# Self attention of a two-block transformer kernel: the difference of two probability maps formed ahead of the turn on VectorE, in place of products with scaled identities on TensorE

## The reference

```python
def one_block(args):
    q_blk, i = args
    sc = jnp.einsum("bhcqd,bhckd->bhcqk", q_blk, k).astype(jnp.float32) * scale
    qpos = i * Q_BLOCK + jnp.arange(Q_BLOCK)
    mask = kpos[None, :] <= qpos[:, None]
    sc = jnp.where(mask, sc, -jnp.inf)
    p = jax.nn.softmax(sc, axis=-1)
    a = p[:, :, 0] - lam * p[:, :, 1]
    return jnp.einsum("bhqk,bhkv->bhqv", a.astype(v.dtype), v)
```

## Time and profile before

| | us |
|---|---|
| median of 3 runs | 2945.64 |
| lowest and highest run | 2942.72, 2948.58 |
| the profiled execution, its own time | 2947.96 |
| its span in the profile | 2946.2 |
| busy: TensorE, VectorE, ScalarE, GpSimd | 2858.0, 2019.0, 1037.2, 1740.7 |

### The profile page before, as it was taken

How to read it: one execution, slowest core, us unless ns; L and a number is a source line. 1 busy time by engine, 2 the same in 40 slices (tenths; PEclk the granted TensorE clock), 3 DMA queues, 4 the chain that set the end, 5 groups by cost and what they waited for, 6 DMA issues and landing times.

```text
span 2946.2 us, 40618 instructions
## 1 busy us (share of the span) xinstructions
PE 2858.0 (97%) x15350; PEld 2547.8 (86%) x15350; DVE 2019.0 (69%) x3386; ACT 1037.2 (35%) x1972; POOL 1740.7 (59%) x997
## 2 busy tenths in 40 slices
PE   6999999999999999999999999999999989999999
PEld 5777778888788777778878889999999989999999
DVE  6985459996352634666647589999898956666663
ACT  3153232121122422333341223333356654444443
POOL 4646447767655235521116667888844558778875
PEclk9999999999999999999999999999999999999999
DMA  4222223333332122210003338999977879999994
GB/s 143 86 66 92 79 65 93 94 100 93 93 115 86 36 61 90 84 39 15 22 23 127 102 99 285 339 329 335 324 256 278 297 262 340 338 344 343 342 342 170
DMA packets 196211, 502.87 MB, mean 171 GB/s; under 512 B 15408, under 2 KB 93488, under 8 KB 194480
## 3 DMA queue, kind: packets, MB, share of 16 engines
q1 hardware_dynamic: 73008, 262.64, 27.4%
q0 software_dynamic: 36864, 134.23, 12.1%
q10 hardware_dynamic: 86144, 103.39, 10.4%
HBM read 448.82 MB, written 51.38 MB: 170 GB/s over the span
## 4 chain that ended last, share of the span: by engine, by line
PE 76%; DVE 14%; issue 3%; POOL 2%; ACT 2%; DMA 2%; DVEq 0%; ACTq 0%; SPq 0%; POOLq 0%
PE banks L1745 20%; PE banks L1747 20%; PE banks L1746 20%; DVE sb_sq L2458 4%; PE banks L1029 3%; PE banks L890 2%; POOL sb_wL L1730 2%; PE banks L898 1%; DVE sb_tmp L2468 1%; DVE sb_sq L2456 1%; PE banks L1807 1%; PE banks L1781 1%; PE banks L1783 1%; PE banks L1782 1%; DVE sb_hL L641 1%
## 5 line engine op out<-in xcount | busy, mean ns | idle before, releaser
L1712 POOL TENSOR_TENSOR sb_wL<-sb_raw,sb_wH 128x1024 fp32r<-128x1024 f32 x242 | 589.0, 2434 | 862.5 <-PE banks L1747 815.0
L1745 PE MATMUL banks<-sb_hH,sb_wH 128*128 128x512 f32 (+1 forms) x2040 | 760.7, 373 | 11.4 <-issue 2.3
L1730 POOL TENSOR_TENSOR sb_wL<-sb_raw,sb_wH 128x1024 fp32r<-128x1024 f32 x253 | 609.4, 2409 | 270.8 <-PE banks L1747 264.7
L1747 PE MATMUL banks<-sb_hH,sb_wL 128*128 128x512 f32 (+1 forms) x2040 | 740.8, 363 | 0.0
L1746 PE MATMUL banks<-sb_hL,sb_wH 128*128 128x512 f32 (+1 forms) x2040 | 740.4, 363 | 0.0
L1745 PEld LDWEIGHTS banks<-sb_hH,sb_wH 128*128 128x128 f32 x2040 | 385.0, 189 | 61.9 <-issue 13.2
L1747 PEld LDWEIGHTS banks<-sb_hH,sb_wL 128*128 128x128 f32 x2040 | 384.3, 188 | 41.0
L1746 PEld LDWEIGHTS banks<-sb_hL,sb_wH 128*128 128x128 f32 x2040 | 385.2, 189 | 38.9 <-issue 1.7
L1194 ACT ACTIVATE sb_wH<-sb_raw 128x1024 fp32r<-128x1024 f32 x253 | 267.9, 1059 | 262.2 <-DMA sb_raw<-in_weights 198.7
L1745 PE MATMUL banks<-sb_pz,sb_wH 128*128 128x384 f32 x1024 | 343.3, 335 | 7.2 <-DVE sb_pz L1650 7.2
L1746 PE MATMUL banks<-sb_pz,sb_wH 128*128 128x384 f32 x1024 | 343.0, 335 | 0.0
(11 more groups left out here) (467 smaller groups left out, 5223.6 us busy)
## 6 DMA issues: line engine op xcount, KB each, us to landing
sb_raw<-in_weights SPq DMA_DIRECT2D x495, 512.0 KB
acts<-sb_sq ACTq DMA_DIRECT2D x120, 192.0 KB
gates<-sb_stage ACTq DMA_DIRECT2D x12, 1920.0 KB, 8.5
sb_Ga<-acts ACTq DMA_DIRECT2D x30, 768.0 KB, 8.3
sb_Gt<-gates ACTq DMA_DIRECT2D x30, 768.0 KB
acts<-sb_xT ACTq DMA_DIRECT2D x1, 2048.0 KB, 7.8
sb_xT<-acts ACTq DMA_DIRECT2D x1, 2048.0 KB, 10.2
out_xT<-sb_xT ACTq DMA_DIRECT2D x8, 256.0 KB, 2.4
```

Of the source, the lines that this page charges most:

```text
L1712: nc.gpsimd.tensor_tensor(wL[:, t % LOS, :], raw[:, t % RAWS, :], wH[:, t % HIS, :].bitcast(F32), ALU.subtract).then_inc(sems("weights_lo" ...
L1730: nc.gpsimd.tensor_tensor(wL[:, t % LOS, :], raw[:, t % RAWS, :], wH[:, t % HIS, :].bitcast(F32), ALU.subtract).then_inc(sems("weights_lo" ...
L1745: pe.matmul(out, hi, H, start=start, stop=False)
L1747: return pe.matmul(out, lo, H, start=False, stop=stop)
```

## The change

The turn no longer scales and adds. ScalarE scales the first map in place by its reciprocal. VectorE multiplies the second reciprocal by the weight `sc[:, 6:7]`, and then forms in place the first map plus the second map times that number. TensorE turns the result block by block with `nc.tensor.transpose` (the helper `turn`). The scaled identities and `lam_ident` go. ScalarE's scaling counts on `probs`, so the counts that others wait for become 3 a unit; two small functions give them.

```diff
+        def exponentials_of(u):
+
+            return 3 * u + 1 if u else 2
+
+        def scaled_of(u):
+
+            return min(3 * u + 5, 48)
...
                 def scores(u):
                     h, i = units[u]
-                    E.at("probs", 2 * (u - 1))
+                    E.at("probs", exponentials_of(u - 2) if u >= 2 else 0)
...
                         for kb in range(units[u][1] + 1):
-                            for c in range(2):
-                                mm = nc.tensor.matmul(ps[6][:, kb * P:(kb + 1) * P], B["p"][:, u % 2, c, kb * P:(kb + 1) * P],
-                                                      B["att"][:, u % 2, c * P:(c + 1) * P], start=(c == 0), stop=(c == 1))
+                            mm = turn(ps[6][:, kb * P:(kb + 1) * P], B["p"][:, u % 2, 0, kb * P:(kb + 1) * P])
...
                     E.wait("recip")
-                    E.at("blocks_turned", u - 1)
-                    act.activation(B["att"][:, u % 2, 0:P], ident, ACT.Copy, scale=ss[:, u % 2, 6:7])
-                    act.activation(B["att"][:, u % 2, P:2 * P], lam_ident, ACT.Copy, scale=ss[:, u % 2, 7:8]).then_inc(sems("att"), 1)
+                    first_map = B["p"][:, u % 2, 0, 0:P * (i + 1)]
+                    act.activation(first_map, first_map, ACT.Copy, scale=ss[:, u % 2, 6:7]).then_inc(sems("probs"), 1)
...
-                v.tensor_scalar(lam_ident, ident, sc[:, 6:7], None, ALU.mult)
...
                     taps(SPLIT + 3 * u, SPLIT + 3 * u + 1)
                     o = u % 2
-                    E.wait("probs", 2)
-                    E.at("att", u - 1)
-                    v.reciprocal(ss[:, o, 6:8], ss[:, o, 4:6]).then_inc(sems("recip"), 1)
+                    E.at("probs", exponentials_of(u))
+                    chain(v.reciprocal(ss[:, o, 6:8], ss[:, o, 4:6]))
+                    v.tensor_scalar(ss[:, o, 7:8], ss[:, o, 7:8], sc[:, 6:7], None, ALU.mult).then_inc(sems("recip"), 1)
                     taps(SPLIT + 3 * u + 1, SPLIT + 3 * u + 3)
+                    E.at("recip", u + 1)
+                    E.at("probs", scaled_of(u))
+                    maps = [B["p"][:, o, c, 0:P * (i + 1)] for c in range(2)]
+                    v.scalar_tensor_tensor(out=maps[0], in0=maps[1], scalar=ss[:, o, 7:8], in1=maps[0], op0=ALU.mult,
+                                           op1=ALU.add).then_inc(sems("att"), 1)
```

More of the change, by code:

```diff
@@ L685, in sb_in @@
             return ps[first + min(kb, 2)][:, at:at + qw[kb]]
-        lam_ident = dg[:, 1, S - P:S]
         parts = [(2, slice(offs[2], 1280), slice(0, 1280 - offs[2])), (1, slice(offs[1], offs[2]), slice(0, qw[1])),
@@ L1988, in _ @@
                         h, i = n // TB, n % TB
-                        E.at("probs", 32 + n - 2)
+                        E.at("probs", 48 + n - 2 if n >= 2 else 0)
                         for b in range(2):
@@ L2382, in _ @@
                 chain(v.tensor_tensor(tmp[:, 0, :], tmp[:, 0, :], tmp[:, 1, :], ALU.add))
+                E.n["probs"] = 48
                 E.meet()
```

## The result

| us | before | after |
|---|---|---|
| median of 10 runs | 2945.53 | 2962.30 |
| lowest and highest run | 2939.21, 2948.76 | 2950.89, 2965.12 |
| the profiled execution, its own time | 2947.96 | 2962.46 |
| its span | 2946.2 | 2960.7 |

The changed kernel is slower by a factor of 1.0052, 95% interval 1.0039 to 1.0064, and its median lies above the range of 2945 to 2957. Two of the ten, 2950.89 and 2951.20, lie near the forecast of 2950.2; the other eight took 2958 or more.

The account below looks back on a forecast made before the run. TensorE was taken to bound the self attention, VectorE after the change. 0.55 plus 4.0 us for meetings with GpSimd made +4.6: 2952.6 for the profiled execution, 2950.2 after 2.3 less for the median; range 2945 to 2957.

Parts of the forecast that it names:

- VectorE becomes the bound: Self attention: with the combinations VectorE needs 16.66 us a head, what TensorE took before, so the gain is eaten.
- the 40 turns: Self attention, TensorE: 160 passes go, 40 turns of 0.112 us come; 17.9 us become 4.5, 13.4 less.
- VectorE's steps: Between one combination's end and the next's start: 4.01 us for i = 2; 3.48, 3.75, 3.21 for i = 0, 1, 3.
- The meetings: Combinations with i = 2 stand behind GpSimd's subtraction L1712: +1.12 us each, +0.67 in unit 14, together 4.0 us.
- The row: Trace reading that L641 ended 0.55 us behind GpSimd's subtraction; kept over the exclusive lock, which would add 0.8 us in sum.
- a head's 16.78 us: Self attention before the change: a head of four units costs 16.78 us, all of it TensorE's.
- The forecast's own sign of being wrong: Wrong if a head takes under 16.5 us, i = 0 combinations are stretched, or the clock leaves 1.00 after 162 us.
- +4.6: Whole change: 0.55 us at the next stage's opening product plus 4.0 for meetings with GpSimd.
- the edges 0.55: Reckoning from first combination to next stage's opening product, meetings left out: 226.15 instead of 225.60, +0.55 us.
- I had taken nothing: ScalarE's scaling as a link in units with i = 1: taken as nothing, 0.2 us a head at most.
- the clock rival: Clock falls after TensorE's waits in i = 2 units: 0.5 x 4 = 2 us more, 2952.2; chance 0.14.
- second meeting at i = 0: Rival: combinations with i = 0, 0.6 us later, also fall behind L1712; 8.5 us for three heads, 2958.7; chance 0.12.

Follow-up runs that it names:

- e4: Changed kernel, with identity products nobody reads filling TensorE's waits only from unit 13 on and ahead of the meeting of engines; 2951.14 us.
- e2: Changed kernel, with identity products nobody reads filling TensorE's waits in every unit but the first two and at the stage's end; 2952.71 us.
- e1: Changed kernel, with the combination reading its second input from the tap sum's PSUM bank, leaving the first map out of the result; 2956.97 us.
- e11: Kernel before the change, with ScalarE held up by fourteen waited-for copies ahead of its last copy of turned blocks, in unit 15; 2958.99 us.
- e10: As e9, but with the other form of the combination for units i = 1 and i = 3, same fills; 2944.24 us.
- e12: As e9, but without its filling products; 2949.01 us, ratio 1.0009 to the kernel before.
- e9: Kernel before, i = 3 alone: VectorE adds the second map, ratio-weighted, to the first; TensorE turns by one scaled identity; tail filled; 2942.31 us.
- e3: Kernel before, with the new scaling, combination and turn for units i = 3 alone, the others keeping scaled identities; 2946.74 us.

## Why the prediction was wrong

**Right.** VectorE becomes the bound; the 40 turns; VectorE's steps. From the start of one combination to the next with i = 2 are 187.30 - 182.81 = 4.49 us, and 4.50 were forecast; for i = 3 to i = 0 it is 4.23 in both. A head that meets GpSimd once is 18.08 us long (192.18 to 210.26); 17.8 was forecast, and 0.30 of the difference is a wait for ScalarE's scaling. The meetings come with i = 2 and not with i = 0, 1.65 to 1.67 us long. The combination of 384 columns ended 0.41 us after the subtraction; by the exclusive lock of the Trainium skill (SBUF — State Buffer, "Who interferes with whom") its full 0.62 would have followed. The row decides for the shorter time, as it did ahead. One reading was a little too strong, without a consequence for the sum: a head's 16.78 us before were not all TensorE's, since 1.5 us of the chain in it lie on ScalarE (exponentials 0.87, scalings 0.59).

The forecast's own sign of being wrong, a clock that leaves 1.00 after 162 us, came true as well.

**The account up to the opening product**, +8.3 where +4.6 was forecast:
- three combinations with i = 2 at 1.66 for 0.62 and unit 14's at 1.05: 3.1 + 0.4 = 3.5 (forecast 4.0);
- the edges 0.55, taken over from the forecast: they are what closes the sum, and were not measured apart;
- unit 1's combination (163.72) stood behind the write of the high part (L1714, 163.50 to 164.55) and took 1.10 for 0.48: 0.6, not forecast;
- three waits of the combination for ScalarE's scaling, 0.30, 1.08 and 0.58: 2.0. I had taken nothing, 0.2 a head at most. They go with the low clock (1.8 in e4, none in e2), though e1 has it for less long and none of them. The way from the one to the other is my reading, not measured: a late TensorE makes scores and turned blocks late, ScalarE's copies with them, and the scaling stands behind those;
- the last products, from the end of unit 15's combination to the opening product, 4.88 us where 3.28 was forecast, at a clock of 0.50: 1.6. At full clock e4 takes 3.85 here, with idle products ahead of the last values, so 1.0 of the 1.6 is shown to go with the clock.

Sum 3.5 + 0.55 + 0.6 + 2.0 + 1.6 = 8.3. The last two, 3.6 us, I put down to the clock.

**The failed step** is the clock rival's "0.5 x 4 = 2 more, 2952.2", and with it the sum's silence on everything behind the opening product. I saw the fall coming, named it with a chance of 0.14, and priced it inside the stage alone, against the microsecond that TensorE is ahead of VectorE there. Inside the stage that was nearly the right size, 2.0 in waits, but partly by luck: they were waits for ScalarE's scaling, which I had priced at nothing; and 1.6 at the end I had not counted. The large price lay where TensorE is the bound again. The stage ends on three units in which it has next to nothing to do, the next one opens at 0.50, and its sums and products keep that for another 20 us: 9.7 us, which e4 took away to within 0.1 by filling the last units, and e11 made from nothing in the old kernel (6.8). With it the forecast would have been 2950.2 + 9.7 = 2959.9, near the measured 2962.3. The two runs of the changed kernel at 2951 would fit executions that did not pay this price; no profile was taken of one.

**Which rivals held.** No second meeting at i = 0. A clock that "falls after each of these waits" is nearly right, but the waits needed no meeting: e1 has none and loses the clock. What stays open is why one execution loses the clock under the opening sums (e10, e12, briefly e1 and e2) and another does not (the kernel before, e9): for the changed kernel the runs show that filling makes it rarer (e2, e4), not when it is safe. What in the next stage keeps the clock down for 20 us was not tried.

## What to carry to other kernels

When work is taken off the engine that is the bound, look past the end of the stage: the granted clock of TensorE in the stretch behind is part of the price, and a tail that leaves it idle can cost more there than all that was saved (here 13.4 us of TensorE's work removed, 16.8 us lost). Cost a clock that falls where TensorE is the bound, not where it waits anyway. And when one engine's spare time (2.7 us a head here) is to take over another's work, move only as much as fits, with no third engine in the chain: moving the widest unit alone ended the stage 2.0 us early (e3), and 3.7 without ScalarE's scaling in the chain (e9); moving all four ended it 8.3 late. Neither e3 nor e9 is shown to be faster than the kernel before as a whole.

## What the runs showed of the hardware

- The half clock can last although TensorE is busy nearly all the time: 0.50 over 24 us in which TensorE was busy 22.2 (the changed kernel from 228 us), 17 us at 15.9 busy (e11), and 20 us at 20.0 busy in e12, where the fall itself came 3 us into a stage that had opened at 1.00. In the changed kernel's own stage it came back after 3 to 7 us (190 to 193, 207 to 214), with keys, scores and values to compute.
- Thirty-one products of the identity by itself, 0.22 us each, kept it at 1.00 from 212 us to L555 in e4's profile; in e2's the clock fell for 3 to 4 us behind the opening for all the filling.
- GpSimd's single-input write of the high part meets a combination too. It (L1714) takes 1.36 us when it begins during a combination, 1.05 when the combination comes after it; and VectorE can stand behind that write as well (unit 1, 1.10 us for 0.48). An instruction of VectorE that starts at the same moment as the subtraction loses: 2.48 us for 128 columns (e2).
